# Attention steps of a two-layer diffusion trunk: the MLA transposes ahead of the diff values, and in odd steps the MLA values right behind the MLA scores

## The reference

```
def _sdpa(q, k, v, scale):                       # MLA
    s = einsum('bqhd,bkhd->bhqk', q, k) * scale
    return einsum('bhqk,bkhd->bqhd', softmax(s), v)

def _diff_sdpa(q1, q2, k1, k2, v, scale, lam):   # diff
    p1 = softmax(einsum('bqhd,bkhd->bhqk', q1, k1) * scale)
    p2 = softmax(einsum('bqhd,bkhd->bhqk', q2, k2) * scale)
    return einsum('bhqk,bkhd->bqhd', p1 - lam * p2, v)
```

## Time and profile before

| | |
|---|---|
| median of three runs | 2873.28 us (2872.22 to 2878.89) |
| the profiled execution, its own time | 2874.66 us |
| its span in the profile | 2872.9 us |
| busy: PE, PEld, DVE, ACT | 2814.1 (98%), 2422.1 (84%), 1666.0 (58%), 886.6 us (31%) |
| mean granted clock of TensorE | 0.993 of 2.4 GHz |
| first attention, 808 to 952 us: PE, DVE, ACT busy | 133.8, 108.1, 95.5 of 144 us |
| second attention, 2318 to 2430 us: PE, DVE, ACT busy | 106.6, 85.8, 73.5 of 112 us |

### The profile page before, as it was taken

How to read it: one execution, slowest core, us unless ns; L and a number is a source line. 1 busy time by engine, 2 the same in 40 slices (tenths; PEclk the granted TensorE clock), 3 DMA queues, 4 the chain that set the end, 5 groups by cost and what they waited for, 6 DMA issues and landing times.

```text
span 2872.9 us, 43910 instructions
## 1 busy us (share of the span) xinstructions
PE 2814.1 (98%) x16966; PEld 2422.1 (84%) x16966; DVE 1666.0 (58%) x3114; ACT 886.6 (31%) x1378; POOL 106.9 (4%) x82
## 2 busy tenths in 40 slices
PE   6999999999999999999999999999999999999998
PEld 4888888888866788888888888888889867898997
DVE  5876588743557578767777335433434566543443
ACT  4221122232366442211223322122233366422223
POOL 0000000025000000000000000000006000000000
PEclk8999999999999999999999999999999999999999
DMA  6443343423300134433432223221214300333332
GB/s 230 124 132 115 112 124 120 128 58 82 89 17 1 32 115 124 125 117 106 133 121 92 59 66 102 82 66 58 74 56 101 88 22 1 89 89 101 88 96 80
DMA packets 425677, 259.68 MB, mean 90 GB/s; under 512 B 27073, under 2 KB 418857, under 8 KB 425578
## 3 DMA queue, kind: packets, MB, share of 16 engines
q1 hardware_dynamic: 425072, 258.20, 30.3%
q10 hardware_dynamic: 506, 0.13, 0.0%
HBM read 251.88 MB, written 2.10 MB: 88 GB/s over the span
## 4 chain that ended last, share of the span: by engine, by line
PE 94%; DVE 3%; ACT 1%; issue 1%; DMA 1%; SPq 0%; DVEq 0%; ACTq 0%
PE pair L756 57%; PE pair L750 27%; PE pair L1049 2%; PE pair L1002 1%; PE pair L1017 1%; PE pair L1026 1%; PE pair L718 1%; PE pair L1034 1%; PE pair L979 1%; DVE n_lo L1541 0%; DVE mod_acc L1677 0%; DVE lo_w L1502 0%; PE pair L967 0%; PE pair L972 0%; DMA x_tok<-in_ctx 0%
## 5 line engine op out<-in xcount | busy, mean ns | idle before, releaser
L756 PE MATMUL pair<-n_hi,hi_w 128*128 128x260 f32 (+2 forms) x3456 | 847.0, 325 | 12.2 <-DVE n_lo L1541 6.6
L756 PE MATMUL pair<-n_hi,lo_w 128*128 128x258 f32 (+2 forms) x3456 | 842.4, 324 | 0.0
L756 PE MATMUL pair<-n_lo,hi_w 128*128 128x256 f32 (+1 forms) x3456 | 842.0, 324 | 0.0
L756 PEld LDWEIGHTS pair<-n_hi,hi_w 128*128 128x128 f32 x3456 | 531.9, 189 | 74.2 <-DVE lo_w L1502 6.6
L756 PEld LDWEIGHTS pair<-n_hi,lo_w 128*128 128x128 f32 x3456 | 534.3, 189 | 57.2
L756 PEld LDWEIGHTS pair<-n_lo,hi_w 128*128 128x128 f32 x3456 | 533.5, 189 | 56.2
L1502 DVE TENSOR_TENSOR lo_w<-raw_w,hi_w 128x1024 fp32r<-128x1024 f32 (+1 forms) x296 | 394.6, 1333 | 291.7 <-ACT hi_w L1138 290.9
L1138 ACT CAST hi_w<-raw_w 128x1024 fp32r<-128x1024 f32 (+1 forms) x296 | 328.9, 1111 | 661.4 <-PE pair L756 363.3
L1677 DVE SCALAR_TENSOR_TENSOR mod_acc<-mod_w,silu_c,mod_acc 128x256 f32<-128x256 f32 x896 | 364.6, 478 | 0.0
L1600 DVE TENSOR_TENSOR buf<-pair,rstd 128x512 f32<-128x512 f32 (+1 forms) x308 | 164.7, 570 | 305.5 <-PE pair L756 305.5
L750 PE MATMUL pair<-h_hi,hi_w 128*128 128x512 f32 x1232 | 338.9, 345 | 0.0
(11 more groups left out here) (194 smaller groups left out, 1925.0 us busy)
## 6 DMA issues: line engine op xcount, KB each, us to landing
raw_w<-in_ffn_w SPq DMA_DIRECT2D x176, 512.0 KB, 3.8
mod_w<-in_w_mod SPq DMA_DIRECT2D x64, 1024.0 KB, 5.1
raw_w<-in_ffn_w SPq DMA_DIRECT2D x64, 704.0 KB, 4.6
raw_w<-in_w_in SPq DMA_DIRECT2D x38, 512.0 KB, 4.1
raw_w<-in_w_out SPq DMA_DIRECT2D x16, 512.0 KB, 3.8
pro_scale<-in_w_mod SPq DMA_DIRECT2D x2, 2048.0 KB, 15.8
pro_shift<-in_w_mod SPq DMA_DIRECT2D x2, 2048.0 KB, 13.4
x_tok<-in_x SPq DMA_DIRECT2D x4, 512.0 KB, 5.5
```

Source lines behind the costliest of these rows:

```text
L756: mm = pe.matmul(pair[s][:, a:a + m], wt[:, k * P:(k + 1) * P], src[:, of(k):of(k) + m], start=opens, stop=closes)
```

## The change

On TensorE, in each step of the attention, the MLA values move from the end of the step to right behind the MLA scores, and the MLA transposes go ahead of the diff values. On ACT, in even steps, the copy of the MLA probabilities goes ahead of out_diff. No instruction, wait or buffer is added or taken away; DVE's and the DMAs' queues stay.

```diff
--- before.py
+++ after.py
@@ -1058,11 +1058,11 @@
                         transposes_diff(c - 1)
                     if c < n_steps:
                         scores_mla(c)
-                    if c:
-                        values_diff(c - 1)
-                        transposes_mla(c - 1)
                     if c % 2 and c >= 3:
                         values_mla(L, c - 2)
+                    if c:
+                        transposes_mla(c - 1)
+                        values_diff(c - 1)
 
             for q, w in enumerate(SWEEPS):
                 if starts_norm(w):
@@ -1397,10 +1397,10 @@
                         high_mla(c - 3)
                     if c < n_steps:
                         exponential(c, 1)
+                    if c and c % 2 == 0:
+                        probabilities_mla(c - 1)
                     if c:
                         out_diff(c - 1)
-                    if c and c % 2 == 0:
-                        probabilities_mla(c - 1)
                     if c < n_steps:
                         if c:
                             act.wait_ge(t_mla, st0 + c)
```

## The result

The changed kernel takes 2935.86 us (median of four runs, 2934.10 to 2938.74) against 2872.86 us of the kernel before beside it. The ratio is 1.0217, with a 95% interval from 1.0205 to 1.0230: 63 us or 2.2% slower.

The account below looks back on a forecast made before the run. TensorE, busy 98% of the span, was taken to bound the kernel. Waits of 58 us and clock falls of 6 add 64 to the profiled 2874.7 or median 2873.3: 2937 us forecast, range 2900 to 2970 for 8 in 10.

Parts of the forecast that it names:

- two stalls: Odd step: TensorE idles 1.76 us before the MLA values; the even step's second half of diff scores idles about 1.5.
- The first stall: Odd steps from 3 on: moved MLA values wait at L714 for the exponential of half 1, 1.76 us each.
- The late diff values: Odd steps: out_diff waits for the diff values and starts at 9.49 where it was 5.33.
- a second stall: Even step: second half of the diff scores waits for scale_mla (L1864), about 1.5 us.
- A pair of steps: Odd and even step with 768 keys: 16.9 us where it was 13.44, so +3.5 us.
- The last 0.4: Next odd step: second half of the scores waits for out_diff, late from ACT's even-step reorder, 0.4 us.
- The short steps: First pass, around 256-key steps: 4.15 us for steps 9 and 11, 8.3 for four; key changes +3.4 each.
- The term of the waits, 58 us: Both attention passes: 38.5 for eleven pairs, 10.2 at key changes, 8.3 for 256-key steps, 1 for step 1.
- The term of the clock, 6 us: TensorE's clock falls behind one in four of 14 first stalls, 1.65 us each; bounds 0 and 23 us.
- The rule behind that term: TensorE: first stalls of 1.76 us are shorter than the shortest idle seen to lower the clock, 1.87.
- only the first stall is paid: Rival: out_diff or turn_inverse has unseen slack, so the second half of the scores doesn't wait; 2899 us, chance 0.12.
- The clock falls in every pair: Rival: TensorE's clock falls in each pair; 2954 us, or 2977 if second stalls lower it too, chance 0.22.

Follow-up runs that it names:

- Kernel 4: Against kernel 3, DVE takes the maximum of half 1 ahead of the pt_diff copy in odd steps with MLA values: 2888.6 us.
- kernel 7: Changed kernel with keys from 512 on left out of half 1 of the diff attention and without the wait at L714: 2897.9 us, ratio 1.0084.
- kernel 3: Changed kernel with ACT's odd steps reordered: turn_inverse and MLA probabilities before the MLA exponential, out_diff last: 2912.0 us, ratio 1.0127.
- Kernel 9: Changed kernel with seven filler matmuls ahead of the MLA values, in odd steps with 768 keys alone: 2930.7 us, ratio 1.0197.
- kernel 2: Kernel before with the MLA values moved behind the MLA scores in odd steps, without the swap, ACT's old order: 2931.2 us, ratio 1.0206.
- kernels 8: Changed kernel with seven filler matmuls ahead of the MLA values in each odd step from 3 on: 2931.3 us, ratio 1.0199.
- kernel 6: Changed kernel with keys from 512 on left out of half 1 of the diff attention, wait at L714 kept: 2921.6 us, ratio 1.0161.
- Kernel 5: Kernel before with keys from 512 on left out of half 1 of the diff attention (scores, maximum, exponential): 2873.3 us, ratio 1.0000.

## Why the prediction was right

2937 us was forecast, 2935.9 measured, and the mechanism of the waits is the one forecast: two stalls, at the places and from the engines named. Two of the sizes, that of the waits and that of the clock, were off in opposite directions and made up for each other. That it came within about 1 us is luck.

- **The first stall** was forecast at 1.76 us and is 1.76 us, in front of L718, ended by L1358. Kernel 4 moved it by the exponential of half 1, kernel 7 took it away.
- **The late diff values** were to bring out_diff to 9.49 of the odd step and a second stall. It is at 9.58 and the stall is there, ended by L1864. Kernels 3 and 7 show it to be a loss of its own. Its size was off: 1.11 us of idle where about 1.5 was forecast. Part of that is the count: the idle begins at the end of the record of the first piece, 1.13 us behind its start, and the forecast counted from 0.9. For the rest, I had taken 0.66 for out_diff and 0.99 from the exponential to turn_inverse; the trace after has 0.60 and 0.88 (2400.36, 2400.96, 2401.84).
- **A pair of steps** was forecast at 16.9 and is 16.52, so 3.08 us longer and not 3.5. The last 0.4, out_diff late for the next odd step (L999), is 0.23: those scores take 1.72 us up to the next block where they took 1.49.
- **The short steps**: steps 9 to 12 took 16.2 us and take 19.4, 3.2 more where 4.15 was forecast. Steps 19 and 20 took 12.9 and take 17.3, 4.4 more where 3.4 was.
- **The term of the waits, 58 us, was too large.** Kernel 9's two passes, with 5 us more at 0.5 inside them than before, are 53.4 us longer. Half of the 5 at most is the clock's, so the waits are 51 to 53.
- **The term of the clock, 6 us, was too small.** The changed kernel's passes are 61.3 us longer in the profiled execution, so 8 to 10 are the clock's. Kernel 9 gives back 7.9. The term had one fall for four of the 14 first stalls, 3.5 falls of 1.65 us. There are three, of 1.61, some 5 us: this count held. It left out the other waits. The wait for the MLA probabilities, which the sum has at the changes of keys and at the end of the second pass, is 2.00 and 2.63 us there, longer than the 1.87 that I had as the shortest idle to lower the clock, and I counted no fall for it. More than half of the time at 0.5 lies in those steps and in the last one of the first pass.
- **The rule behind that term was wrong.** I had four idles of the trace before, of which two lowered the clock. The same trace has another fall, in the last step of the second pass, behind two shorter idles close together:

```profile
2424.14 0.85 PE L1026 MATMUL pair<-ident,buf 128*128 128x128 f32 x6 [1.16 <-ACT proj L1376]
2426.04 2.42 PE L1049 MATMUL pair<-v_tok,proj 128*128 128x128 f32 x12 [1.05 <-DVE proj L1882]
```
```profile
2426.00:2427.00 1.00, 0.96 (x7) 0.96 (x8) 0.05 (x1) 0.00 (x0) 0.00 (x0) 0.82 0.00 0
```

The granted clock is 0.82 in that window and 0.50 in the next, so 1.87 was not the shortest. The same stall had falls behind it in three of 14 places in the changed kernel, five of 14 in kernel 2 and nine of 14 in kernel 3, so that three where 3.5 were counted is luck as well. The profiled execution has the lowest mean clock of the four, 0.988 where the others have 0.990; what the clock took in those is not known.

Three small slips changed nothing: the 21.6 us of the earlier trace rows are loads and matmuls together and not loads alone, the windows of the fall at 1054 add up to 3.4 us and not 3.3, and the bounds of pair and clock together give 2912 to 2960 us and not 2918 to 2956.

Of the rivals, "only the first stall is paid" (2899) is refuted by kernels 3 and 7. "The clock falls in every pair" (2954) did not come: in the changed kernel it falls behind three of the 14 stalls. The nine of 14 in kernel 3 say that it was a near rival. "Not slower" needed exp_done[1] when the MLA scores are through; kernel 7 grants just that, by other data, and is still 25 us slower than its base, of which the clock can have 10. So that rival's condition would not have been enough: I had named only the one wait, and there are two.

By the Trainium skill, "TensorE: Matmul & The Clock Gate", section "A second HAM failure mode: psum-queue depth-cycling", frequent short idles between groups of matmuls make the clock swing. The trace agrees: 20 us at 0.5 went with the filler. That most of the stalls of one length did not lower the clock in the changed kernel, 11 of 14, is what the trace adds.

Left open: which of the stalls of one length lower the clock, and whether the 2 us between kernels 8 and 9 are more than chance. The waits for the MLA probabilities have no experiment of their own; kernel 3 takes them away together with the second stall.

## What to carry to other kernels

Before a block is moved ahead in an in-order queue, read two things off the trace: when each of its waits ends at the new place, and what hangs on the blocks that it is put ahead of. Here each was worth about half of the loss in the kernels with fewer keys (6 and 7), and the wait that it was to fill was worth 0.2 us a pair. A stall of 1.8 us on TensorE where it sets the end can cost its length and, where the clock falls behind it, nearly as much again.

## What the runs showed of the hardware

- Kernel 5 leaves out the second piece of half 1 of the scores, 256 columns over 64 rows, and its steps stay at 7.56 and 5.88 us. I had expected 0.2 us less, and 2864 us. The group in front of the transposes is 1.55 us with 6 matmuls where it was 1.56 with 8: the code puts the two halves in different rows of the array (64 each), and they stream side by side, so leaving one out saves nothing. The MLA scores say the same: they have half as many columns to stream, over 96 rows, and take 1.46 us.

```profile
2361.40 1.55 PE L1004 MATMUL pair<-proj 64*128 64x512 f32 x6
```

- The same idle lowers the granted clock in some steps and not in others. Of the 14 first stalls with 768 keys, 1.74 to 1.79 us long, three had a fall behind them in the changed kernel, five in kernel 2 and nine in kernel 3. With the idle at 1.26 to 1.32 us (kernel 6), at 0.89 to 0.95 us (kernel 4) or filled (kernels 8 and 9) none of the 14 had. Length alone doesn't decide: behind the stall of 1.04 us in step 23 of the changed kernel the clock fell, to 0.50 in the window from 985 to 986, with another idle of 1.15 us some 5 us ahead of it.
